# Q, K and V of an attention layer as three products of rounded halves in place of fp32 products

## The chip, the cores and the metric

The kernel is one program on one core of a Trainium2 chip. It is timed in device microseconds (us) of that core; the number that counts is the median of several executions.

## What is computed

Two decoder layers over 256 tokens of width 1024. Layer 0 is a state-space mixer and a dense SwiGLU; layer 1 is a stick-breaking attention (16 heads of 64) and a routed SwiGLU with eight experts, two for each token. Each sub-layer is normalised before and after, and modulated by a vector c. The change touches the projection to Q, K and V:

```python
def stick_breaking_attention(h, w_qkv, w_out):
    qkv = (h @ w_qkv).reshape(bsz, seq, 3, SB_HEADS, SB_HEAD_DIM)
    ...
    z = jnp.einsum("bhqd,bhkd->bhqk", q[:, :, t0:n_keys], k[:, :, :n_keys]) * scale
    ...
    return o @ w_out
```

h is 256 x 1024 and w_qkv is 1024 x 3072, all in fp32.

## The kernel before

All weights come through a ring of seven slots (`ring`, 2 MB each). SyncE issues the loads of the whole kernel in one fixed order (`load`, L485 to L488); a load waits until TensorE has counted `used` for the slot's last content. The granules (one filling of a slot each) that matter here are numbered: 46 to 51 are w_qkv (two for Q, two for K, two for V, 512 columns each), 52 and 53 are the output projection, 54 to 57 the last four of the modulation weights, and from 58 on come the experts' weights. The first five of the experts' granules are loaded without knowing the routing; every later one waits for `route_done` (L550).

The order of each engine's work is written out by hand. Around the change TensorE does this: the last down product of the dense SwiGLU (L2295 to L2308), two modulation products (`ada`, L2336), transposes of the normalised rows (`transpose_x`, L2338), `wait_hT`, then the four granules of Q and K (L2342 to L2354), the two of V (L2355 to L2362), then the heads (L2403 to L2409), the output projection (L2416), modulation, router, gather, and the experts.

- Q and K: for each granule four blocks of 128 output columns, each eight fp32 products over k. The weights are the stationary operand (128 x 128) and `hT`, the transposed activations, is the moving one with 256 columns. That is 128 products, and the profile records each as two loads and two matmuls. The result of a granule stands in banks 0, 1 or 2, 3 of PSUM by turns, and ScalarE copies it to `qT` or `kT` (L890).
- V: for each granule two blocks of 128 tokens, each eight fp32 products with the activations stationary and 512 columns of weights moving: 32 products. VectorE copies them to `v_sb` (L1543).
- Before them ScalarE and VectorE write `hT` (L685 and L1265). ScalarE reads two modulation results (`ada_mod(8)`, `ada_mod(9)`, L712), and loads a table of functions (L886).

The dense SwiGLU before and the experts' main products after are already done the other way. `w_round` (L759 on ScalarE) writes the rounded value of half a granule, as type fp32r, to a buffer; `w_rest` (L1470 on VectorE) writes what the rounding left, over the granule itself (`ring_lo` has the same addresses as `ring`, `x_lo` the same as `hT`); the activations are split the same way (L858, L1514). `split_product` (L2266) then makes one product of three fp32r matmuls: high x high, high x low, low x high.

Of the kernel before, what the change touches and what calls it, by code (L numbers as in the profile page):

```python
# [26 lines left out]
F32 = mybir.dt.float32  # L27
F32R = mybir.dt.float32r
I32 = mybir.dt.int32
U32 = mybir.dt.uint32  # L30
ALU = mybir.AluOpType
ACT = mybir.ActivationFunctionType
AX = mybir.AxisListType

P = 128
D = 1024
KD = D // P
SEQ = 256
TT = SEQ // P
# [7 lines left out]
DH = 64  # L47
# [7 lines left out]
RING = 7  # L55
GRAN = 4096
# [6 lines left out]
G_BANK, U_BANK, T_BANK, S_BANK, Y_BANK = 0, 1, 2, 3, 4  # L63
# [44 lines left out]
N_QKV = 46  # L108
# [29 lines left out]
def program(nc, x, c, ada_w, ada_b, norm_g, s5_w_in, s5_lambda_re, s5_lambda_im, s5_b_re, s5_b_im,  # L138
# [3 lines left out]
    with ctx:  # L142
        def sb(name, shape, dt=F32):
            return ctx.enter_context(nc.sbuf_tensor(name, shape, dt))

        def sem(name):
            return ctx.enter_context(nc.semaphore(name))

        ps = ctx.enter_context(nc.psum_tensor("ps", [P, 8, 512], F32))
# [10 lines left out]
        half = sb("half", [P, 1])  # L160
# [14 lines left out]
        with ExitStack() as first:  # L175
            ring, hT, gg, junk, tbuf, arena = (first.enter_context(nc.sbuf_tensor(name, shape, F32)) for name, shape in (
                ("ring", [P, RING, GRAN]), ("hT", [P, KD, SEQ]), ("gg", [P, D]), ("junk", [P, D]), ("tbuf", [P, D]),
                ("arena", [P, ARENA])))
        with ExitStack() as second:
            def sb2(name, shape):  # L180
                return second.enter_context(nc.sbuf_tensor(name, shape, F32))

            ring_lo = [sb2(f"ring_lo{i}", [P, GRAN]) for i in range(RING)]
            x_lo = sb2("x_lo", [P, KD, SEQ])
            sb2("rows_between", [P, 3 * D])
            w_hi, x_hi = sb2("w_hi", [P, 2, GRAN]), sb2("x_hi", [P, KD, SEQ])
            aT_hi, aT_lo = sb2("aT_hi", [P, 2, 4, P]), sb2("aT_lo", [P, 2, 4, P])
        sb("ring_kept", [P, RING, GRAN])
        w3 = sb("w3", [P, 3, GRAN // 2])
        x3_hi, x3_lo = sb("x3_hi", [P, KD, P]), sb("x3_lo", [P, KD, P])  # L190
# [12 lines left out]
        class Place:  # L203
# [37 lines left out]
        qT, kT, oT = pl(KD, SEQ), pl(KD, SEQ), pl(KD, SEQ)  # L241
# [62 lines left out]
        whi_done, wlo_done, xhi_done, xlo_done, ahi_done = (  # L304
            sem("whi_done"), sem("wlo_done"), sem("xhi_done"), sem("xlo_done"), sem("ahi_done"))
        qk_done, v_out = sem("qk_done"), sem("v_out")
        z_ps, zabs_done, zcopy_done, exp_done, ln_done, sp_done, spm_done = (
            sem("z_ps"), sem("zabs_done"), sem("zcopy_done"), sem("exp_done"), sem("ln_done"), sem("sp_done"),
            sem("spm_done"))
# [57 lines left out]
        def gran(n):  # L367
            return ring[:, n % RING, :]

        def gran8(n):  # L370
            return gran(n).rearrange("p (k n) -> p k n", k=KD)
# [4 lines left out]
        def wait_landed(eng, n, turn=None):  # L376

            eng.wait_ge(landed[n % RING], 16 * (n // RING if turn is None else turn) + 16)

        def wait_used(eng, n, turn=None):  # L380

            eng.wait_ge(used[n % RING], (n // RING if turn is None else turn) + 1)

        def ff_half(buffer, half):
            return buffer[:, 2048 * half:2048 * half + 2048]
# [40 lines left out]

        def half3(h):
            return w3[:, h % 3, :]

        def pair_kinds(eng):  # L430

# [219 lines left out]
        def _(act):  # L651
# [27 lines left out]
            def hT_evict(s, parts=(0, 1, 4, 5)):  # L679

                act.wait_ge(mod_done, s + 1)
                for k in parts:
                    act.wait_ge(hT_ps, 4 * s + k // 2 + 1)
                    dst, src = turned(s, k)
                    act.activation(dst, src, ACT.Identity, bias=shift_col(s, k), scale=scale_c[:, s, k:k + 1]  # L685
                                   ).then_inc(hT_act, 1)
# [22 lines left out]
            def ada_mod(i):  # L709

                act.wait_ge(mod_ps, i + 1)
                act.activation(modc[:, i // 6, 2 * (i % 6):2 * (i % 6) + 2, :],  # L712
                               ps[:, ada_bank(i), 0:8].rearrange("p (q r) -> p r q", r=2), ACT.Copy
                               ).then_inc(mod_out, 1)
# [166 lines left out]
            pre_stats(2)  # L881
            ada_part(9)
            hT_evict(2)
            ada_mod(8)
            ada_mod(9)
            act.preload_act_table_set("natural_log_exp_and_others")  # L886
            for r in range(4):
                wait_used(act, N_QKV + r)
                src = ps[:, 2 * (r % 2):2 * (r % 2) + 2, :].rearrange("p a (b n) -> p (a b) n", b=2)
                act.activation((qT if r < 2 else kT)[:, 4 * (r % 2):4 * (r % 2) + 4, :], src, ACT.Copy,  # L890
                               scale=DH ** -0.5 if r < 2 else 1.0).then_inc(qk_done, 1)
            def o_out(h):
                act.wait_ge(o_ps, h + 1)
                act.activation(oT[:, h, :], ps[:, 6 + h % 2, 0:256], ACT.Copy).then_inc(o_done, 1)
# [325 lines left out]
        def _(dve):  # L1220
# [316 lines left out]
            to_hT(2)  # L1537
            hT_evict(2)

            for n in range(2):  # L1540
                wait_used(dve, N_QKV + 4 + n)
                for tt in range(TT):
                    dve.tensor_copy(v_sb[:, tt, 512 * n:512 * n + 512], ps[:, Y_BANK + 2 * tt + n, :]  # L1543
                                    ).then_inc(v_out, 1)
# [507 lines left out]
        def _(pe):  # L2052
# [51 lines left out]
            def wait_hT(s):  # L2104
                pe.wait_ge(hT_act, 4 * s + 4)
                pe.wait_ge(hT_dve, 4 * s + 4)
# [159 lines left out]
            def split_product(dst, stationary, moving, start, stop):  # L2266

                for i, (a, b) in enumerate(((0, 0), (0, 1), (1, 0))):
                    ins = pe.matmul(dst, stationary[a].bitcast(F32R), moving[b].bitcast(F32R),  # L2269
                                    start=start and i == 0, stop=stop and i == 2)  # L2270
                return ins
# [67 lines left out]
            ada_fold(8)  # L2339
            ada_fold(9)  # L2340
            wait_hT(2)
            for r in range(4):  # L2342
                n = N_QKV + r
                wait_landed(pe, n)
                above(pe, qk_done, r - 1)
                if r == 0:
                    pe.wait_ge(gg_done, 2)
                for j in range(4):
                    if r == 0 and j == 2:
                        pe.wait_ge(mod_out, 10)  # L2350
                    for k in range(KD):
                        ins = pe.matmul(ps[:, 2 * (r % 2) + j // 2, 256 * (j % 2):256 * (j % 2) + 256],  # L2352
                                        gran8(n)[:, k, P * j:P * j + P], hT[:, k, :], start=k == 0, stop=k == KD - 1)
                ins.then_inc(used[n % RING], 1)  # L2354
            for r in range(2):  # L2355
                n = N_QKV + 4 + r
                wait_landed(pe, n)
                for tt in range(TT):
                    for k in range(KD):
                        ins = pe.matmul(ps[:, Y_BANK + 2 * tt + r, :], tokens(k, tt), gran8(n)[:, k, :],  # L2360
                                        start=k == 0, stop=k == KD - 1)
                ins.then_inc(used[n % RING], 1)  # L2362

            def scores(h):

# [680 lines left out]
```

## Time and profile before

| | |
|---|---|
| median of 3 executions | 1531.9 us (1530.35 to 1533.28) |
| the profiled execution | 1534.63 us, its span 1532.9 us |
| TensorE matmuls busy | 1383.5 us (90%) |
| TensorE weight loads busy | 976.7 us (64%) |
| VectorE busy | 661.3 us (43%) |
| ScalarE busy | 498.7 us (33%) |
| moved by DMA | 474.28 MB, mean 309 GB/s |
| mean granted clock of TensorE | 0.949 of 2.4 GHz |

The span runs from the first to the last instruction; the execution's own time is 1.7 us longer. A matmul's recorded duration includes its passage through the array, so its real cost in a row of many is the distance between two starts. "busy" is the union of the recorded spans. A granted clock of 1.00 means 2.4 GHz, 0.50 means 1.2 GHz.

### The profile page before, as it was taken

The numbers are of one execution on the slowest core, as the hardware profiler recorded it, in microseconds if no ns is written. First come the engines' busy times: TensorE is split into PE (matmuls) and PEld (weight loads), VectorE is DVE, ScalarE is ACT, GpSimd is POOL, SyncE is SP. The second block draws the span as 40 slices with busy tenths as digits, with TensorE's granted clock in tenths as the row PEclk, the third lists the DMA queues.
The fourth block names the chain that finished last, engine by engine and source line by source line (L and its number), as shares of the span: only waits on it lengthen the run. The fifth ranks groups of instructions, "written<-read, shape, count | busy, mean of one in ns | idle before, by whom it ended". The sixth has DMA issues, their size and how long they took to land.

```text
span 1532.9 us, 25160 instructions
## 1 busy us (share of the span) xinstructions
PE 1383.5 (90%) x11083; PEld 976.7 (64%) x11084; DVE 661.3 (43%) x755; ACT 498.7 (33%) x557; POOL 34.8 (2%) x66
## 2 busy tenths in 40 slices
PE   3999999999999789899999899999797888988687
PEld 2763788888686545677777577767575565544343
DVE  5943444454400634765544555544665353200003
ACT  2323433434300512444443354433454352000001
POOL 2001000000100002000000000000000000000000
PEclk8989999999999998999999999999998899999889
DMA  8784884554664114559999969999989999999994
GB/s 296 298 316 176 314 346 165 196 188 169 244 246 165 55 51 170 204 216 410 411 411 413 406 234 410 412 410 414 410 340 412 411 412 413 410 411 413 412 413 171
DMA packets 206792, 474.28 MB, mean 309 GB/s; under 512 B 9986, under 2 KB 10030, under 8 KB 206670
## 3 DMA queue, kind: packets, MB, share of 16 engines
q1 hardware_dynamic: 199968, 470.83, 79.0%
q10 hardware_dynamic: 6702, 1.71, 0.5%
q8 instruction: 91, 1.49, 0.4%
q14 instruction: 31, 0.25, 0.0%
HBM read 471.47 MB, written 1.05 MB: 308 GB/s over the span
## 4 chain that ended last, share of the span: by engine, by line
PE 66%; DMA 14%; SPq 11%; DVE 4%; ACT 2%; issue 1%; ACTq 1%; POOL 0%; DVEq 0%
PE ps L2269 34%; SPq L488 11%; DMA ring<-in_moe_w_down_dram 10%; PE ps L2550 7%; PE ps L2562 5%; PE ps L2352 4%; DMA ring<-in_moe_w_gate_up_dram 2%; DMA ring<-in_ada_w_dram 2%; PE ps L2416 2%; PE ps L2245 2%; PE ps L2360 2%; PE ps L2080 2%; DVE ring_lo L1836 1%; DVE arena L1235 1%; PE ps L2144 1%
## 5 line engine op out<-in xcount | busy, mean ns | idle before, releaser
L1836 DVE TENSOR_TENSOR ring_lo<-ring,w 128x2048 fp32r<-128x2048 f32 x126 | 288.4, 2289 | 196.1 <-ACT w L1005 154.1
L1005 ACT ACTIVATE w<-ring 128x2048 fp32r<-128x2048 f32 x126 | 240.6, 1913 | 233.4 <-PE ps L2269 209.3
L2550 PE MATMUL ps<-ring,arena 128*32 128x128 f32 (+1 forms) x5376 | 253.2, 299 | 40.6 <-DMA ring<-in_moe_w_gate_up_dram 32.8
L2550 PEld LDWEIGHTS ps<-ring,arena 128*32 128x32 f32 (+1 forms) x5376 | 189.8, 117 | 104.7 <-issue 45.0
L2269 PE MATMUL ps<-ring_lo,x_hi 128*128 128x512 f32 x560 | 219.4, 392 | 0.0
L2269 PE MATMUL ps<-w,x_hi 128*128 128x512 f32 x336 | 136.4, 406 | 7.1 <-DVE arena L1783 5.5
L1475 DVE TENSOR_TENSOR ring_lo<-ring,w_hi 128x2048 fp32r<-128x2048 f32 x42 | 95.6, 2290 | 85.9 <-ACT w_hi L765 85.9
L2269 PE MATMUL ps<-w,x_lo 128*128 128x512 f32 x336 | 132.1, 393 | 0.0
L2269 PEld LDWEIGHTS ps<-ring_lo,x_hi 128*128 128x128 f32 x560 | 105.9, 189 | 20.3
L2562 PE MATMUL ps<-ring,tri 128*32 128x512 f32 (+1 forms) x448 | 75.7, 693 | 28.0 <-DMA ring<-in_moe_w_down_dram 26.5
L765 ACT ACTIVATE w_hi<-ring 128x2048 fp32r<-128x2048 f32 x42 | 78.8, 1909 | 50.3 <-PE ps L2269 42.1
L2269 PE MATMUL ps<-w_hi,x_hi 128*128 128x512 f32 x224 | 89.4, 399 | 0.0
L2269 PEld LDWEIGHTS ps<-w,x_hi 128*128 128x128 f32 x336 | 63.8, 190 | 37.4 <-issue 18.2
L2269 PE MATMUL ps<-w_hi,x_lo 128*128 128x512 f32 x224 | 87.3, 390 | 0.0
L2269 PE MATMUL ps<-w,a_hi 128*128 128x512 f32 x168 | 69.9, 416 | 2.8 <-DVE a_lo L1871 2.8
L2269 PEld LDWEIGHTS ps<-w,x_lo 128*128 128x128 f32 x336 | 63.6, 189 | 13.7
L2269 PE MATMUL ps<-ring_lo,a_hi 128*128 128x512 f32 x168 | 67.0, 399 | 0.0
L2269 PE MATMUL ps<-w,a_lo 128*128 128x512 f32 x168 | 66.7, 397 | 0.0
L2562 PE MATMUL ps<-ring,arena 128*32 128x512 f32 (+1 forms) x336 | 53.6, 615 | 9.9 <-DMA ring<-in_moe_w_down_dram 7.7
L2080 PE MATMUL ps<-ring,c 128*32 128x512 f32 x384 | 50.4, 678 | 13.1 <-DMA ring<-in_ada_w_dram 12.8
L2562 PEld LDWEIGHTS ps<-ring,tri 128*32 128x32 f32 (+1 forms) x448 | 18.8, 125 | 60.5 <-DMA ring<-in_moe_w_down_dram 30.1
L2352 PE MATMUL ps<-hT,ring 128*128 128x256 f32 x256 | 57.2, 387 | 0.0
(391 smaller groups left out, 1560.6 us busy)
## 6 DMA issues: line engine op xcount, KB each, us to landing
ring<-in_moe_w_gate_up_dram SPq DMA_DIRECT2D x112, 2048.0 KB, 17.2
ring<-in_moe_w_down_dram SPq DMA_DIRECT2D x56, 2048.0 KB, 18.2
ring<-in_ada_w_dram SPq DMA_DIRECT2D x24, 2048.0 KB, 10.8
ring<-in_ffn_w_gate_up_dram SPq DMA_DIRECT2D x14, 2048.0 KB, 12.2
ring<-in_ffn_w_down_dram SPq DMA_DIRECT2D x7, 2048.0 KB, 7.9
ring<-in_sb_w_qkv_dram SPq DMA_DIRECT2D x6, 2048.0 KB, 8.6
ring<-in_s_w_out_dram SPq DMA_DIRECT2D x2, 2048.0 KB, 7.7
ring<-in_sb_w_out_dram SPq DMA_DIRECT2D x2, 2048.0 KB, 13.7
```

Source lines behind the costliest of these rows:

```text
L488: sp.dma_start(dst, src).then_inc(landed[n % RING], 16)
L765: act.activation(ff_half(w_hi[:, g % 2, :], half).bitcast(F32R), ff_half(gran(ff_place(g)), half), ACT.Copy).then_inc(whi_done, 1)
L1005: act.activation(half3(h).bitcast(F32R), ff_half(gran(pair_place(*main_granule(n))), half), ACT.Copy).then_inc(whi_done, 1)
L1475: dve.tensor_tensor(ff_half(ring_lo[(ff_place(g)) % RING][:, :], half).bitcast(F32R), w, ff_half(w_hi[:, g % 2, :], half), ALU.subtract).t ...
L1836: dve.tensor_tensor(ff_half(ring_lo[place % RING][:, :], half).bitcast(F32R), ff_half(gran(place), half), half3(h), ALU.subtract).then_inc ...
L2080: ins = pe.matmul(ps[32 * j:32 * j + 32, ada_bank(i), :], c32[:, 4 * part_k + k, :], gran8(places[r])[:, 4 * part_k + k, :], start=k == 0, ...
L2245: ins = pe.matmul(ps[:, 2 * i + half, :], yT[:, k, P * tt:P * tt + P], gran4(WOUT_PLACES[half])[:, k, 512 * n:512 * n + 512], start=k == 0 ...
L2269: ins = pe.matmul(dst, stationary[a].bitcast(F32R), moving[b].bitcast(F32R), start=start and i == 0, stop=stop and i == 2)
L2352: ins = pe.matmul(ps[:, 2 * (r % 2) + j // 2, 256 * (j % 2):256 * (j % 2) + 256], gran8(n)[:, k, P * j:P * j + P], hT[:, k, :], start=k == ...
L2360: ins = pe.matmul(ps[:, Y_BANK + 2 * tt + r, :], tokens(k, tt), gran8(n)[:, k, :], start=k == 0, stop=k == KD - 1)
L2550: ins = pe.matmul(dst[width * r:width * r + width, 0:cols], x[:, k, 0:width], weights[:, k, cols * r:cols * r + cols], start=k == 0, stop= ...
L2562: ins = pe.matmul(ps[width * r:width * r + width, bank, :], a[:, j, 0:width], weights[:, j, 512 * h:512 * h + 512], start=first and i == 0 ...
```

## The change

Each granule of w_qkv is split in halves of four k each (twelve halves, numbered 0 to 11), and eleven of them are done with three fp32r matmuls in place of an fp32 product. Half 0 (k 0 to 3 of Q's first granule) stays plain fp32. Half 1 is the first split one. Rounded halves go by turns to `wq0` and `wq1`, two new buffers of 2048 columns in space that is free before the heads; what the rounding left is written over the granule. ScalarE writes `x_hi` and the rounded weights, VectorE `x_lo` and the rests. `x_lo` for k 0 to 3 lies over `hT`, so it waits until the plain half has been read (`plain_done`). The two `ada_mod` and the load of the table come later in ScalarE's order. The results of Q and K now stand in four banks each, 4 to 7 and 0 to 3 by turns, so V (in banks 4 to 7) waits for the third copy to `kT`.

```diff
@@ scalar
             hT_evict(2)
+            act.wait_ge(hT_act, 12)
+            act.wait_ge(hT_dve, 12)
+            def q_x(half):
+                k = slice(4 * half, 4 * half + 4)
+                act.activation(x_hi[:, k, :].bitcast(F32R), hT[:, k, :], ACT.Copy).then_inc(q_xhi, 1)
+            def q_round(h):
+                n, half = divmod(h, 2)
+                wait_landed(act, N_QKV + n)
+                if h >= 3:
+                    if half:
+                        wait_used(act, N_QKV + n - 1)
+                    else:
+                        act.wait_ge(q_half, n - 1)
+                act.activation(half_q(h).bitcast(F32R), ff_half(gran(N_QKV + n), half), ACT.Copy).then_inc(q_whi, 1)
+            q_x(1)
+            q_round(1)
+            q_x(0)
             ada_mod(8)
             ada_mod(9)
-            act.preload_act_table_set("natural_log_exp_and_others")
-            for r in range(4):
+            def qk_out(r):
                 wait_used(act, N_QKV + r)
...
+            for h in range(2, 12):
+                q_round(h)
+                if h % 2 and h < 10:
+                    qk_out((h - 3) // 2)
+                if h == 2:
+                    act.preload_act_table_set("natural_log_exp_and_others")
@@ vector
             hT_evict(2)
+            def q_x_rest(half):
+                k = slice(4 * half, 4 * half + 4)
+                dve.wait_ge(q_xhi, 2 - half)
+                if not half:
+                    dve.wait_ge(plain_done, 1)
+                dve.tensor_tensor(x_lo[:, k, :].bitcast(F32R), hT[:, k, :], x_hi[:, k, :], ALU.subtract).then_inc(q_xlo, 1)
+            def q_rest(h):
+                dve.wait_ge(q_whi, h)
+                dve.tensor_tensor(low_q(h).bitcast(F32R), ff_half(gran(N_QKV + h // 2), h % 2), half_q(h), ALU.subtract
+                                  ).then_inc(q_wlo, 1)
+            q_x_rest(1)
+            q_rest(1)
+            q_x_rest(0)
+            for h in range(2, 12):
+                q_rest(h)
@@ tensor
             for r in range(4):
-                n = N_QKV + r
-                wait_landed(pe, n)
+                wait_landed(pe, N_QKV + r)
                 above(pe, qk_done, r - 1)
...
-                    for k in range(KD):
-                        ins = pe.matmul(ps[:, 2 * (r % 2) + j // 2, 256 * (j % 2):256 * (j % 2) + 256],
-                                        gran8(n)[:, k, P * j:P * j + P], hT[:, k, :], start=k == 0, stop=k == KD - 1)
-                ins.then_inc(used[n % RING], 1)
+                base = 0 if r % 2 else Y_BANK
+                for half in range(2):
+                    if r + half:
+                        hi, low = q_weights(2 * r + half)
+                        pe.wait_ge(q_xlo, 1 if r == 0 else 2)
+                    for j in range(4):
+                        for i in range(KD // 2):
+                            k = KD // 2 * half + i
+                            dst, cols_j = ps[:, base + j, 0:256], slice(P * j, P * j + P)
+                            if r + half:
+                                ins = split_product(dst, (hi[:, i, cols_j], low[:, i, cols_j]),
+                                                    (x_hi[:, k, :], x_lo[:, k, :]), k == 0, k == KD - 1)
+                            else:
+                                ins = pe.matmul(dst, gran8(N_QKV)[:, k, cols_j], hT[:, k, :], start=k == 0, stop=False)
...
             for r in range(2):
-                n = N_QKV + 4 + r
...
+                pe.wait_ge(qk_done, 3)
+                for half in range(2):
+                    hi, low = q_weights(8 + 2 * r + half)
+                    for tt in range(TT):
+                        for i in range(KD // 2):
+                            k = KD // 2 * half + i
+                            t = slice(P * tt, P * tt + P)
+                            ins = split_product(ps[:, Y_BANK + 2 * tt + r, :], (x_hi[:, k, t], x_lo[:, k, t]),
+                                                (hi[:, i, :], low[:, i, :]), k == 0, k == KD - 1)
+                    q_read(ins, 4 + r, half)
```

## Rows read from the trace of the kernel before

**Rows 1.** The page, 40 slices of the span: busy share of DMA, and its GB/s.

```profile
DMA  8784884554664114559999969999989999999994
GB/s 296 298 316 176 314 346 165 196 188 169 244 246 165 55 51 170 204 216 410 411 411 413 406 234 410 412 410 414 410 340 412 411 412 413 410 411 413 412 413 171
```

**Rows 2.** Busy time of each engine by stretch (us from the start: length, engines).

```profile
core 0: us, PE busy (x) PEld busy (x) DVE busy (x) ACT busy (x) POOL busy (x), PEclk, DMA share, GB/s
418.50:475.70 57.20, 57.20 (x258) 50.09 (x258) 0.00 (x0) 4.53 (x5) 0.23 (x1) 0.97 0.61 224
475.70:503.00 27.30, 27.30 (x65) 11.81 (x63) 1.29 (x2) 1.02 (x1) 0.00 (x0) 1.00 0.43 154
503.00:551.00 48.00, 33.49 (x225) 26.35 (x224) 36.01 (x52) 28.21 (x40) 0.00 (x0) 0.89 0.12 45
```

**Rows 3.** The chain that ended last, longest pieces, from QKV on: start, us, what.

```profile
418.54 57.17 PE ps L2352 x256
475.71 27.47 PE ps L2360 x64
551.07 8.83 PE ps L2416 x16
561.62 20.61 PE ps L2416 x48
```

**Rows 4.** Issues of the DMA queue by time: start, us, queue.

```profile
380.94 35.54 SPq L488 DMA_DIRECT2D ring<-in_sb_w_qkv_dram  x6
416.52 18.15 SPq L488 DMA_DIRECT2D ring<-in_sb_w_out_dram  x2
503.20 82.98 SPq L488 DMA_DIRECT2D ring<-in_moe_w_gate_up_dram  x4
```

**Rows 5.** What the DMA queue waited for, whole span: us, times, longest.

```profile
SPq L457 <- DVE cnt_i L1710: 31.3, 1, 31.3
```

**Rows 6.** TensorE in order of time, last 32 matmuls of Q and K.

```profile
468.64 7.07 PE L2352 MATMUL ps<-hT,ring 128*128 128x256 f32 x32
```

**Rows 7.** The chain in the dense SwiGLU: runs of fp32r matmuls, 512 columns each.

```profile
262.55 27.53 PE ps L2269 x120
290.52 5.50 PE ps L2269 x24
```

**Rows 8.** TensorE matmuls and weight loads (PEld) in order of time, same stage.

```profile
386.18 0.39 PE L2269 MATMUL ps<-w_hi,aT_hi 128*128 128x512 f32 x1
386.19 0.19 PEld L2269 LDWEIGHTS ps<-ring_lo,aT_hi 128*128 128x128 f32 x1
386.41 0.39 PE L2269 MATMUL ps<-ring_lo,aT_hi 128*128 128x512 f32 x1
```

**Rows 9.** The chain, fp32 matmuls narrow enough that the loads set the pace.

```profile
878.12 3.52 PE ps L2505 x32
```

**Rows 10.** The same 128 narrow matmuls' weight loads: ns min, median, max; times; form.

```profile
L2505 PEld LDWEIGHTS ps<-arena,hn x128: 186/192/192, 645.6 to 1319.1; 128*128 128x128 f32 x128
```

**Rows 11.** The chain, a run of fp32r matmuls in the experts' stage.

```profile
786.68 5.67 PE ps L2269 x24
```

**Rows 12.** Rounding and rest instructions of the dense SwiGLU: ns min, median, max; times; form.

```profile
L858 ACT ACTIVATE x_hi<-hT x2: 1058/1059/1060, 161.3 to 163.3; 128x1024 fp32r<-128x1024 f32 x2
L1514 DVE TENSOR_TENSOR x_lo<-hT,x_hi x2: 1225/1226/1226, 162.4 to 164.4; 128x1024 fp32r<-128x1024 f32 x2
L765 ACT ACTIVATE w_hi<-ring x42: 1895/1909/1919, 118.0 to 382.8; 128x2048 fp32r<-128x2048 f32 x42
L1475 DVE TENSOR_TENSOR ring_lo<-ring,w_hi x42: 2284/2292/2295, 120.0 to 385.2; 128x2048 fp32r<-128x2048 f32 x42
```

**Rows 13.** Copies of Q and K, and of V: ns min, median, max; times; form.

```profile
L890 ACT ACTIVATE arena<-ps x4: 1023/1023/1023, 434.3 to 475.7; 128x1024 f32<-128x1024 f32 x4
L1543 DVE COPY arena<-ps x4: 681/686/692, 489.5 to 503.8; 128x512 f32<-128x512 f32 x4
```

**Rows 14.** The chain, a rounding followed by its rest in the experts' stage.

```profile
1080.46 1.92 ACT w L1005
1082.40 4.50 DVE ring_lo L1836 x2
```

**Rows 15.** ScalarE in order of time where Q's first product starts.

```profile
418.57 0.18 ACT L712 ACTIVATE modc<-ps 128x8 f32<-128x8 f32 x1 [0.28 <-PE ps L2090]
418.77 1.28 ACT L886 ACT_TABLE_LOAD   x1
```

More of the change, by code:

```diff
@@ L187, in program, with sb3 @@
             aT_hi, aT_lo = sb2("aT_hi", [P, 2, 4, P]), sb2("aT_lo", [P, 2, 4, P])
+        with ExitStack() as third:
+            def sb3(name, shape):
+                return third.enter_context(nc.sbuf_tensor(name, shape, F32))
+            sb3("before_o", [P, RING * GRAN + KD * SEQ + 3 * D + 2 * KD * SEQ])
+            wq0 = sb3("wq0", [P, GRAN // 2])
+            sb3("values_third", [P, 2 * KD * SEQ])
+            wq1 = sb3("wq1", [P, GRAN // 2])
         sb("ring_kept", [P, RING, GRAN])
@@ L306, in program @@
         qk_done, v_out = sem("qk_done"), sem("v_out")
+        q_xhi, q_xlo, q_whi, q_wlo, q_half, plain_done = (
+            sem("q_xhi"), sem("q_xlo"), sem("q_whi"), sem("q_wlo"), sem("q_half"), sem("plain_done"))
         z_ps, zabs_done, zcopy_done, exp_done, ln_done, sp_done, spm_done = (
@@ L428, in half3, with half_q, low_q @@
             return w3[:, h % 3, :]
+        def half_q(h):
+            return (wq0, wq1)[h % 2][:, :]
+        def low_q(h):
+            return ff_half(ring_lo[(N_QKV + h // 2) % RING][:, :], h % 2)
         def pair_kinds(eng):
@@ L883, in _ @@
             hT_evict(2)
+            act.wait_ge(hT_act, 12)
[15 more added lines that the diff above has]
+            q_x(0)
             ada_mod(8)
             ada_mod(9)
-            act.preload_act_table_set("natural_log_exp_and_others")
-            for r in range(4):
+            def qk_out(r):
                 wait_used(act, N_QKV + r)
-                src = ps[:, 2 * (r % 2):2 * (r % 2) + 2, :].rearrange("p a (b n) -> p (a b) n", b=2)
-                act.activation((qT if r < 2 else kT)[:, 4 * (r % 2):4 * (r % 2) + 4, :], src, ACT.Copy,
-                               scale=DH ** -0.5 if r < 2 else 1.0).then_inc(qk_done, 1)
+                base = 0 if r % 2 else Y_BANK
+                act.activation((qT if r < 2 else kT)[:, 4 * (r % 2):4 * (r % 2) + 4, :], ps[:, base:base + 4, 0:256],
+                               ACT.Copy, scale=DH ** -0.5 if r < 2 else 1.0).then_inc(qk_done, 1)
+            for h in range(2, 12):
[4 more added lines that the diff above has]
+                    act.preload_act_table_set("natural_log_exp_and_others")
             def o_out(h):
@@ L2341, in _, with q_weights, q_read @@
             wait_hT(2)
+            def q_weights(h):
+                pe.wait_ge(q_wlo, h)
+                return [w.rearrange("p (k n) -> p k n", n=512) for w in (half_q(h), low_q(h))]
+            def q_read(ins, n, half):
+                ins.then_inc(used[(N_QKV + n) % RING] if half else q_half, 1)
             for r in range(4):
-                n = N_QKV + r
-                wait_landed(pe, n)
+                wait_landed(pe, N_QKV + r)
                 above(pe, qk_done, r - 1)
-                if r == 0:
+                if r == 1:
@@ L2347, in _ @@
                     pe.wait_ge(gg_done, 2)
-                for j in range(4):
-                    if r == 0 and j == 2:
-                        pe.wait_ge(mod_out, 10)
-                    for k in range(KD):
-                        ins = pe.matmul(ps[:, 2 * (r % 2) + j // 2, 256 * (j % 2):256 * (j % 2) + 256],
-                                        gran8(n)[:, k, P * j:P * j + P], hT[:, k, :], start=k == 0, stop=k == KD - 1)
-                ins.then_inc(used[n % RING], 1)
-            for r in range(2):
-                n = N_QKV + 4 + r
[L2357 to L2362, printed above, removed]
+                    pe.wait_ge(mod_out, 10)
@@ new lines, in _ @@
+                base = 0 if r % 2 else Y_BANK
+                for half in range(2):
[11 more added lines that the diff above has]
+                                ins = pe.matmul(dst, gran8(N_QKV)[:, k, cols_j], hT[:, k, :], start=k == 0, stop=False)
+                    if r + half:
+                        q_read(ins, r, half)
+                    else:
+                        ins.then_inc(plain_done, 1)
```

## The prediction

> **What bounds the kernel now.** I read the slices of the page first. From the nineteenth slice on the DMA engines move some 410 GB/s almost without a pause: the experts' stage is tied to the stream of weights. In slices 14 and 15, the heads, they move 55 and 51 GB/s [rows 1]: there the stream waits for TensorE. So the question is whether time saved at Q, K and V moves the start of the late stream, or is swallowed by it. The busy times by stretch answer the first half: from 418.5 to 503.0 us TensorE is busy all the time, VectorE nearly idle (0.00 and 1.29 us), ScalarE 4.53 and 1.02 us, and DMA at 0.61 and 0.43 [rows 2]. The chain of waits says the same: it runs through all 57.17 us of Q and K and all 27.47 us of V, then through the heads and the output projection [rows 3]. The DMA queue answers the second half: the six granules of w_qkv are issued by 416.5 us, and the first of the experts' loads goes out at 503.20 us, when V's last product is done; the fourth and later ones follow the output projection [rows 4]. The loads after the fifth wait 31.3 us for the routing, which VectorE computes at the end of the chain [rows 5]. Nothing after V is tied to an absolute time. A microsecond taken from Q, K and V is a microsecond off the end, the heads and everything behind them simply start earlier.
>
> **Q and K, matmuls.** Before: 128 products, 256 recorded matmuls, 57.17 us [rows 3]. The last 32 records take 7.07 us from the first start to the last end; less 0.38 us for the last one's passage, 31 distances of 0.216 us [rows 6]. 256 of these are 55.3 us; the other 1.9 us are the start of the stage, at a granted clock of 0.97 on average [rows 2], and stay, since the first products are the same. After: the 16 plain products of half 0 are 32 records, 6.9 us, with the start 8.8 us. The other 112 products are 336 fp32r matmuls of 256 columns. No row shows an fp32r matmul as narrow as that, so this price is bounded from both sides. In the dense SwiGLU 120 fp32r matmuls of 512 columns take 27.53 us, 24 take 5.50 us: 0.229 us each [rows 7]; two successive starts lie 0.23 us apart [rows 8]. 512 columns at 2.4 GHz would be 0.213, so 0.016 us come on top, whether per matmul or per column is open. With 256 columns the stream is 0.107 us, and with all of the 0.016 on top 0.123. From below, the pace of the loads is a floor: 32 fp32 matmuls of 64 columns, each with a load of 128 x 128, take 3.52 us, 0.110 us each, though their own two passes need only 0.053 [rows 9]. I take 0.121, near the upper end, as part of the 0.016 (the seams between groups) should not repeat with each matmul: 336 x 0.121 = 40.7 us. The floor of 0.110 gives 37.0. Under the traffic of the experts' stage the wide ones take 5.67 / 24 = 0.236 us [rows 11], 0.007 more; 0.130 for the narrow ones is the upper bound, 43.7 us.
>
> **V, matmuls.** Before: 32 products, 27.47 us [rows 3]. After: 96 fp32r matmuls of 512 columns, the form that rows show: 96 x 0.229 = 22.0 us [rows 7], at most 96 x 0.236 = 22.7 [rows 11].
>
> **Sum.** Before 57.17 + 27.47 = 84.6 us; after 8.8 + 40.7 + 22.0 = 71.5. That is 13.1 us less: 7.7 from Q and K, 5.4 from V. By the bounds the gain is 16.8 (floor of the loads) to 9.4 us (both upper prices).
>
> The page "TensorE: Matmul & The Clock Gate" of the Trainium skill gives, under "Back-to-back issue gap", N / 2.4 + 2.5 ns for N columns. That would be 0.216 us at 512 columns, and the fp32r rows are 0.013 over it [rows 7], so the trace doesn't agree for this type; by the page the two stages would save 18.4 us, an estimate from its formula.
>
> **The split operands, what hides them.** None of ScalarE's and VectorE's new work is on the path as long as it is done before TensorE asks. I count from TensorE's first product. The durations are those of the same instructions in the dense SwiGLU: `x_hi` 1.06 us, `x_lo` 1.23, rounding of half a granule 1.91, its rest 2.29 [rows 12].
> - ScalarE: `x_hi` for k 4 to 7 until 1.1, rounding of half 1 until 3.0, `x_hi` for k 0 to 3 until 4.1, then the two `ada_mod` at 0.18 each, rounding of half 2 until 6.4, then the table, 1.28 [rows 12, 15].
> - VectorE: `x_lo` until 2.4, rest of half 1 until 5.4. TensorE wants it at 8.8: 3.4 us of cover. Then `x_lo` for k 0 to 3 waits for the plain half; VectorE stands in that wait with the rest of half 2 queued behind it: 8.8 + 1.2 + 2.3 = 12.4. TensorE wants it when half 1 is done, at 8.8 + 48 x 0.121 = 14.6: 2.2 us of cover.
> - From half 3 on a buffer is free when TensorE has done the half two before, and rounding and rest must be done within the half between: 1.91 + 2.29 = 4.2 us and the handovers, against 5.8 us for Q and K (48 matmuls) and 24 x 0.229 = 5.5 for V. A rest follows its rounding by 0.02 us [rows 14]; with some 0.1 to 0.3 us for each signal to and from TensorE the margin is about 1 us.
> - The copies of Q and K (1.02 us [rows 13]) stand behind a rounding in ScalarE's order, so they come 1.9 us later than they could. The copy of a granule is asked for one granule later (11.6 us), V needs the third one while the fourth granule is being worked on: covered. If the cover were gone, each would cost about 1.0 us. V's copies stand behind the last rest, which is done some 4.5 us into V's second granule, so they too are ready; the last pair is at the very end, as before.
> - `ada_mod(8)` and `ada_mod(9)` come 4.1 us later. Behind them wait the GpSimd's sum, not wanted for long, and TensorE before Q's second granule, at 14.6 us. Zero. The extra waits of ScalarE for `hT` are those that TensorE ends anyway. No DMA is moved in SyncE's order, and the slots come free once per granule as before, only sooner; w_qkv is issued by 416.5 us, so the third granule has landed long before about 445 us, when it is wanted.
>
> **Rivals.**
> 1. *The weight loads come out from under the short matmuls* (slower). An fp32r product needs three loads for 256 columns each; before, two for the same number of columns twice. If a load kept TensorE for its recorded 0.188 to 0.192 us [rows 10], 336 matmuls would take 0.19 us: 23.2 us more than in my sum, 10 us slower than before, about 1542. If loads and streams simply followed one another, 0.110 + 0.107 = 0.217 each, it would be 32 us over my sum, 1551. It decides for slower from 0.160 us per matmul on (13.1 / 336 = 0.039 over 0.121). Against it: the loads with 192 ns on record follow at 0.110 us [rows 9, 10], and a load starts 0.01 us after the matmul before it starts, long before that one ends [rows 8]. For it: no row has an fp32r load under a stream as short as the load itself. The Trainium skill, "TensorE: Matmul & The Clock Gate", section "Part 3: Packing small matmuls", says that a load overlaps a running matmul only if it aims at other rows of the array; by that rule this rival would be the outcome, and [rows 8] speak against the rule.
> 2. *The narrow fp32r matmul takes as long as the wide one.* Then 336 x 0.229 = 76.9, 36 us over my sum: 1555. The fp32 rows scale with the columns: 0.216 us for 256, 27.47 / 64 = 0.429 for 512 [rows 3, 6]. For fp32r nothing in the trace shows the scaling.
> 3. *The rounding is the bound.* If signals, or ScalarE and VectorE being slower beside TensorE's reading, stretch the 4.2 us to 6.6 per half of Q and K, each of eight halves or so costs 0.8 and V's four 1.1: 11 less 0.1, about 1529. A stretch to 6.0 costs 4 us. Against: the same instructions took at most 1.92 and 2.30 us beside the same matmuls [rows 12].
> 4. *The gain is taken back later*, if the late stream starts by something else than TensorE: 1530 to 1533. [rows 4, 5] speak against.
>
> **How the numbers follow.** Profiled execution: span 1532.9 - 13.1 = 1519.8, time 1534.63 - 13.1 = 1521.5. The median stood 2.7 us under the profiled one, so 1531.9 - 13.1 = 1518.8. Chances: forecast 0.68 (1515 to 1522.5 by its bounds), rival 1 0.09 (0.06 at 1542, 0.03 at 1551), rival 2 0.06, rival 3 0.10, rival 4 0.07. The forecast with its spread and that of the executions reaches from 1514 to 1524; rival 3 and a part of rival 4 are taken in up to 1530, which leaves rivals 1 and 2 out and holds about 0.8. A measurement can tell 0.2%, 3 us, from no change. Faster by more than that: forecast and most of rival 3, 0.77. Within: rival 4 and the rest, 0.08. Slower: rivals 1 and 2, 0.15.
>
> **What would show it.** In the profile after: 336 matmuls of 256 columns on `split_product`'s line, about 0.12 us apart; rest of half 2 ended before half 1; no idle time of TensorE put down to the new rests between 418 and 490 us; V's 96 at 0.229; the first of the experts' loads at about 490 us in place of 503.20, and the end as much earlier. What would make it wrong is the narrow fp32r matmul above all: each 0.01 us is 3.4 us of the end. Next is a margin at the buffers smaller than 1 us, seen as idle time every half.

## The result

The changed kernel takes 1520.32 us (median of 5, 1517.84 to 1523.64) against 1533.28 us before (median of 5, 1530.35 to 1536.14). The ratio is 0.9907, 95% interval 0.9892 to 0.9922: a gain of under 1%, but clear of the scatter. The profiled execution has a span of 1518.6 us, 14.3 us less than before. In a second set beside other kernels the ratio was 0.9908 (0.9892 to 0.9925), and the span of the profile 1520.8 us.

The chain of waits of the changed kernel, its long pieces from the stage on (start, us, what), to be read beside [rows 3]:

```profile
421.27 8.82 PE ps L2433 x32
430.09 62.09 PE ps L2332 x432
539.97 7.13 PE ps L2502 x16
548.82 20.61 PE ps L2502 x48
```

L2433 is the plain half, L2332 `split_product`: Q, K and V are 8.82 + 62.09 = 70.9 us in place of 57.17 + 27.47 = 84.6. That is 13.7 us. The stretches of the changed kernel are the plain half, the split part of Q and K, and V (columns as in [rows 2]):

```profile
421.20:430.10 8.90, 8.90 (x35) 7.53 (x35) 3.52 (x2) 7.01 (x7) 1.26 (x1) 0.81 1.05 407
430.10:470.50 40.40, 40.40 (x338) 40.36 (x338) 17.18 (x8) 14.23 (x10) 0.00 (x0) 1.00 0.61 227
470.50:492.30 21.80, 21.80 (x98) 17.80 (x98) 8.15 (x6) 6.66 (x4) 0.00 (x0) 1.00 0.54 193
```

TensorE has no pause in any of the three. In the middle one the weight loads count as busy for 40.36 of 40.40 us too. That alone doesn't make them the limit: each is recorded with 0.19 us, and where one starts every 0.120 us the records overlap and fill the whole stretch. VectorE and ScalarE, nearly idle there before, now work 28.8 and 27.9 us under TensorE. The matmuls and loads of `split_product` between 430 and 492 us (times in ns, min, median, max), and what TensorE waited for at them:

```profile
L2332 PE MATMUL ps<-x_hi,wq x112: 280/283/472, 429.7 to 469.9; 128*128 128x256 f32 x112
L2332 PEld LDWEIGHTS ps<-x_lo,wq x112: 187/192/192, 429.9 to 469.9; 128*128 128x128 f32 x112
L2332 PE MATMUL ps<-wq,x_hi x32: 389/389/396, 470.2 to 491.3; 128*128 128x512 f32 x32
its engine sat idle before it (us, times) until:
who waited for it (us, times):
  ACT wq L916: 34.1, 9
```

Under "sat idle" stands nothing. The loads are recorded with 192 ns, like those of [rows 10], but the 336 matmuls came 40.4 / 336 = 0.120 us apart. The DMA queue shows that what follows moved along. The first of the experts' loads goes out at 492.22 us, against 503.20 us in [rows 4]:

```profile
383.66 35.60 SPq L504 DMA_DIRECT2D ring<-in_sb_w_qkv_dram  x6
492.22 81.17 SPq L504 DMA_DIRECT2D ring<-in_moe_w_gate_up_dram  x4
```

One profile alone can mislead by 1 to 3 us. Here the stage began 2.7 us later than before, in code that the change doesn't touch; the stage gave 13.7; what follows it was 3.3 us shorter (1026.4 against 1029.7 us). In the second profile the same three are 1.5, 13.7 and -0.2. The stage is the same to 0.1 us, the rest scatters. Only one part of the rest was the same in both: the output projection ran at a granted clock of 1.00 in place of 0.95 and took 29.5 in place of 31.2 us. These are its stretches, before and changed:

```profile
551.07:582.20 31.13, 31.13 (x72) 13.46 (x76) 1.22 (x1) 0.00 (x0) 0.00 (x0) 0.95 0.19 68
```

```profile
539.97:569.40 29.43, 29.43 (x72) 12.89 (x76) 1.23 (x1) 0.00 (x0) 0.00 (x0) 1.00 0.20 72
```

In the kernel before, the granted clock was 1.00 in the last 2 us of the heads, and 0.65 and then 0.50 in the first two stretches of 2 us of the projection; in the changed kernel it stayed at 1.00. The first 16 matmuls of the projection took 7.13 us in all three profiles that have the changed kernel's Q, K and V unaltered ahead of them (the third is that of the last experiment), and 8.2 to 9.3 us in the nine others, one of which is the changed kernel with 20 us of other work put before Q. So the 1.7 us repeat, but whether the change brings them, by the moment at which it lets the projection start, no run says. They can't be told in the time either: behind the projection the two profiles of the changed kernel have 949.2 and 952.8 us against 950.7 before, and the medians gained 13.0 and 13.4 us, while the interval of the first ratio (12.0 to 16.5 us) holds 13.7 + 1.7 too.

### The profile page after: what moved, and what is told of

Its sections match the earlier page's. It is cut to its first block, busy times and chain, and to the rows that moved or that the text cites. A ratio compares the mean times of both kernels' runs of the same rounds, so it can differ in the third digit from the quotient of the medians.

```text
span 1518.6 us, 25494 instructions
## 1 busy us (share of the span) xinstructions
PE 1370.0 (90%) x11227; PEld 981.0 (65%) x11228; DVE 688.5 (45%) x768; ACT 521.2 (34%) x570; POOL 35.8 (2%) x66
## 3 DMA queue, kind: packets, MB, share of 16 engines
q8 instruction: 92, 1.51, 0.4%
## 4 chain that ended last, share of the span: by engine, by line
PE 65%; DMA 15%; SPq 11%; DVE 4%; ACT 2%; issue 2%; ACTq 1%; POOL 0%; DVEq 0%
PE ps L2332 38%; SPq L504 11%; DMA ring<-in_moe_w_down_dram 11%; PE ps L2636 7%; PE ps L2648 5%; DMA ring<-in_ada_w_dram 2%; DMA ring<-in_moe_w_gate_up_dram 2%; PE ps L2308 2%; PE ps L2502 2%; PE ps L2143 2%; DVE arena L1281 1%; PE ps L2207 1%; DVE ring_lo L1899 1%; PE ps L2591 1%; PE ps L2268 1%
## 5 line engine op out<-in xcount | busy, mean ns | idle before, releaser
L2332 PE MATMUL ps<-ring_lo,x_hi 128*128 128x512 f32 x592 | 231.8, 392 | 0.0
L2332 PE MATMUL ps<-w,x_hi 128*128 128x512 f32 x336 | 136.7, 407 | 4.8 <-DVE arena L1846 4.6
L2332 PE MATMUL ps<-w,x_lo 128*128 128x512 f32 x336 | 132.1, 393 | 0.0
L2332 PEld LDWEIGHTS ps<-ring_lo,x_hi 128*128 128x128 f32 x592 | 111.9, 189 | 21.7 <-issue 0.2
L2332 PE MATMUL ps<-w_hi,x_hi 128*128 128x512 f32 x224 | 89.4, 399 | 0.0
L2332 PE MATMUL ps<-w_hi,x_lo 128*128 128x512 f32 x224 | 87.3, 390 | 0.0
L2332 PEld LDWEIGHTS ps<-w,x_hi 128*128 128x128 f32 x336 | 63.7, 190 | 34.3 <-issue 16.0
L2332 PEld LDWEIGHTS ps<-w,x_lo 128*128 128x128 f32 x336 | 63.7, 189 | 13.8
L2332 PE MATMUL ps<-w,a_hi 128*128 128x512 f32 x168 | 69.5, 413 | 2.8 <-DVE a_lo L1934 2.8
L2332 PE MATMUL ps<-w,a_lo 128*128 128x512 f32 x168 | 66.5, 396 | 0.0
L2332 PE MATMUL ps<-ring_lo,a_hi 128*128 128x512 f32 x168 | 66.5, 396 | 0.0
L2143 PE MATMUL ps<-ring,c 128*32 128x512 f32 x384 | 49.9, 673 | 13.7 <-DMA ring<-in_ada_w_dram 13.5
L2648 PEld LDWEIGHTS ps<-ring,tri 128*32 128x32 f32 (+1 forms) x448 | 19.1, 128 | 61.9 <-issue 31.2
L1854 DVE TENSOR_TENSOR c<-c,ps 128x128 f32<-128x128 f32 (+1 forms) x28 | 8.8, 314 | 96.6 <-PE ps L2636 96.6
```

Source lines behind the costliest of these rows:

```text
L2143: ins = pe.matmul(ps[32 * j:32 * j + 32, ada_bank(i), :], c32[:, 4 * part_k + k, :], gran8(places[r])[:, 4 * part_k + k, :], start=k == 0, ...
L2648: ins = pe.matmul(ps[width * r:width * r + width, bank, :], a[:, j, 0:width], weights[:, j, 512 * h:512 * h + 512], start=first and i == 0 ...
```

## The experiments

The theory: each of the two terms (narrow fp32r matmuls in Q and K, wide ones in V) has its price, the rounding is covered, and the whole passes 1:1 to the end. The main rivals: the narrow form or its loads are dear; the plain half isn't needed; the rounding has no margin; later stages take part of the gain back. Where a gain is given beside a ratio, with an interval, it is 1 less the ratio, times the some 1535 us of the kernel before.

**Q and K alone.** V goes back to fp32 products (from the rounded activations, the low part left out).

```diff
-            for h in range(2, 12):
+            for h in range(2, 8):
                 q_rest(h)
...
+                        ins = pe.matmul(ps[:, Y_BANK + 2 * tt + r, :], x_hi[:, k, P * tt:P * tt + P], gran8(n)[:, k, :],
+                                        start=k == 0, stop=k == KD - 1)
```

> Only Q and K are split; V is computed as fp32 products again, from the rounded activations alone (its low part is left out, so V's numbers are coarser). Theory (the two terms of the sum stand alone and pass 1:1 to the end): V's stage takes 27.5 us as before the change, Q and K 49.1 us as in the changed kernel; the time is 5.7 us above the changed kernel's and 7.3 to 8 us under the kernel before. Rival (the gain comes from elsewhere, the later stages in a luckier phase of the clock): the time doesn't follow the stage, the difference to the kernel before is not 7 to 9 us but near 0 or near 13.

```profile
419.31 8.82 PE ps L2434 x32
428.13 40.31 PE ps L2333 x336
468.44 27.47 PE ps L2445 x64
```

The chain has the three parts as expected, 76.6 us, 8.0 less than before. The time: 1528.07 us against 1534.83, ratio 0.9949 (0.9931 to 0.9967), which is 7.8 us (5.1 to 10.6).

**V alone.** Q and K stay fp32; the low part of the activations goes to other space, so nothing is overwritten that Q and K read.

```diff
-                if not half:
-                    dve.wait_ge(plain_done, 1)
-                dve.tensor_tensor(x_lo[:, k, :].bitcast(F32R), hT[:, k, :], x_hi[:, k, :], ALU.subtract).then_inc(q_xlo, 1)
+                dve.tensor_tensor(x_lov[:, k, :].bitcast(F32R), hT[:, k, :], x_hi[:, k, :], ALU.subtract).then_inc(q_xlo, 1)
...
+                            ins = pe.matmul(dst, gran8(N_QKV + r)[:, k, cols_j], hT[:, k, :], start=k == 0, stop=k == KD - 1)
```

> Only V is split; Q and K are fp32 products as before the change (in the four banks each of the changed kernel), and the low part of the activations lies in other space. Theory: Q and K take 57.2 us, V 21.8 us, and the time is 5.4 to 5.7 us under the kernel before. Together with the run that splits Q and K alone the two gains add up to the whole, 13 to 14 us. Rival: they don't add up, since one of them hides the other's rounding: then V alone would stall for its weights and gain under 4 us.

```profile
419.51 57.17 PE ps L2424 x256
476.68 21.78 PE ps L2330 x96
```

57.17 + 21.78 us, no pause before V. Ratio 0.9969 (0.9956 to 0.9983), 4.8 us (2.6 to 6.8) where the stage gives 5.7. In the stage the two gains add up exactly, 8.0 + 5.7 = 13.7; in the times 7.8 + 4.8 = 12.6, within their intervals.

**Half 0 split as well.** No plain half covers the first rounding.

```diff
+            q_x(0)
+            q_round(0)
             q_x(1)
             q_round(1)
-            q_x(0)
```

> Half 0 is split too, so no plain half covers the first rounding. Theory (the plain half is a cover): TensorE stands still for 1.06 + 1.9 + 2.3 = 5.3 us at the start, then works 5.8 us, 11.1 against 8.8 us for the plain half: 2.3 us more than the changed kernel, and up to 1 us more if the clock falls in the pause. Rival (the cover is not needed, other work of ScalarE and VectorE is what TensorE would wait for anyway, and the 32 fp32 records are the dearer way): 8.8 less 5.8, up to 3 us less than the changed kernel.

TensorE's first matmuls after the pause, and the stretch that follows (clock in the column before the last two):

```profile
425.07 0.55 PE L2332 MATMUL ps<-x_hi,wq 128*128 128x256 f32 x1 [5.42 <-DVE ring_lo L1594]
425.42 0.41 PE L2332 MATMUL ps<-x_lo,wq 128*128 128x256 f32 x1
425.63 0.41 PE L2332 MATMUL ps<-x_hi,ring_lo 128*128 128x256 f32 x1
425.84 0.41 PE L2332 MATMUL ps<-x_hi,wq 128*128 128x256 f32 x1
425.00:495.70 70.70, 70.63 (x482) 66.63 (x484) 27.33 (x15) 24.45 (x18) 0.59 (x1) 0.96 0.58 210
```

The pause is 5.4 us, as worked out. But the matmuls after it took 70.56 us, and 62.09 + 5.76 = 67.85 would be their price at full clock; the clock was 0.96. So the stage is 76.0 us, 5.1 over the changed kernel's, not 2.3. The expectation had allowed up to 1 us for the clock; 2.7 us are slow clock. Ratio 0.9963 (0.9952 to 0.9975), 5.7 us under the kernel before.

These 2.7 us are not all the pause's. The stretches of this run (the pause, the slow part) and, in the second fence, of the changed kernel without a pause (just before the stage, its first 3.8 us, the rest of the plain half):

```profile
419.65:425.00 5.35, 0.00 (x0) 0.00 (x0) 3.71 (x3) 5.35 (x4) 0.00 (x0) 0.57 1.05 409
425.00:430.50 5.50, 5.43 (x25) 5.46 (x26) 3.17 (x2) 0.36 (x3) 0.59 (x1) 0.50 1.05 402
```

```profile
419.40:421.20 1.80, 1.80 (x18) 1.78 (x16) 1.76 (x4) 1.56 (x4) 0.00 (x0) 1.00 1.06 413
421.20:425.00 3.80, 3.80 (x11) 3.03 (x11) 2.08 (x2) 3.75 (x4) 0.00 (x0) 0.55 1.06 410
425.00:430.10 5.10, 5.10 (x26) 4.51 (x25) 1.43 (x1) 3.27 (x5) 1.26 (x1) 1.00 1.05 405
```

The clock falls to 1.2 GHz at the start of this stage with and without a pause, in the kernel before too (0.51 from 418.50 to 422.00 us, TensorE busy throughout). The plain half pays 1.9 us for it, 8.82 us where 6.91 are its price at full clock. The pause adds 0.8 us. The 5.1 us are then 5.4 of pause, plus these 0.8, less 1.15, as a split half takes 5.76 us in place of 6.91.

**The pause filled.** To test that the 2.7 us are slow clock and not the operands or the waits, TensorE is kept busy in the pause with products whose result is thrown away.

```diff
             wait_hT(2)
+            for i in range(12):
+                pe.matmul(ps[:, Y_BANK, 0:256], ident[:, :], hn[:, 0, 0:256], start=True, stop=True)
```

> As the run in which all halves are split, but TensorE is kept busy in the pause of 5.4 us by 12 fp32 products of 256 columns whose result is thrown away (24 records, 5.2 us and the cold start). Theory (2.7 us of that run's 76.0 us were a lower clock, which the pause had brought): the 528 matmuls after the pause take 67.9 us in place of 70.6, the stage 73.5 to 75 us. Rival (the 2.7 us come from the operands or from the first half's waits): the stage stays at 76 or gets longer by what the filler runs over.

```profile
418.00 7.01 PE ps L2406 x24
425.01 67.85 PE ps L2332 x480
```

67.85 us, with the clock at 1.00 in that stretch, where 67.9 were expected. So it was the clock. The filler pays for the slow start in its place: 24 records would be 5.2 us at full clock and took 7.0. It runs over the pause by 1.6 us, and still the stage is shorter, 74.9 against 76.0 us. Ratio 0.9942 (0.9925 to 0.9958), 8.9 us (6.5 to 11.5) where the stage gives 9.8. Whatever stands first in this stage pays 1.8 to 1.9 us of slow clock if TensorE works on, and 2.7 us if it pauses first.

**Three roundings in place of one**, from half 3 on.

```diff
+                for i in range(2 if h >= 3 else 0):
+                    act.activation(half_q(h).bitcast(F32R), ff_half(gran(N_QKV + n), half), ACT.Copy).then_inc(again, 1)
+                    act.wait_ge(again, 2 * (h - 3) + i + 1)
                 act.activation(half_q(h).bitcast(F32R), ff_half(gran(N_QKV + n), half), ACT.Copy).then_inc(q_whi, 1)
```

> From half 3 on each rounding is done three times over, 5.8 us in place of 1.9 us, so rounding and rest take 8.2 to 8.5 us of a half that TensorE works on for 5.8 us (5.5 in V). This is the prediction's third rival made real. Theory A, as priced there: every half pays the excess, 9 halves x 2.5 us = 23 us and more over the changed kernel. Theory B: with two buffers the wait goes from one half to the half two before, so a stall at one half gives the next its time, and only every second half pays: 3 x 2.5 + 2 x 2.8 = 13 us, seen as idle times of 2.4 to 3 us at every second half. If the margin were not 1.1 to 1.4 us as the trace has it, both would come out higher or lower by that.

Starts after a pause of TensorE, from its order of time, and its waits from 421 to 510 us in sum:

```profile
444.73 0.39 PE L2336 MATMUL ps<-x_hi,wq 128*128 128x256 f32 x1 [2.53 <-DVE ring_lo L1599]
460.53 0.39 PE L2336 MATMUL ps<-x_hi,wq 128*128 128x256 f32 x1 [2.53 <-DVE ring_lo L1599]
467.33 0.36 PE L2336 MATMUL ps<-x_hi,wq 128*128 128x256 f32 x1 [0.79 <-DVE ring_lo L1599]
```

```profile
PE ps L2336 <- DVE ring_lo L1599: 12.6, 8, 2.5
```

Between the pauses of 2.53 us that end at 444.73 and 460.53 lie two halves of work without one. The sum is theory B's: 12.6 us in all, 13 expected, where theory A asks for 23. Its pattern is not: from 467.33 us on every half pays, in turns less (0.79 to 0.94 us) and more (1.51 to 1.76). What holds is that two halves together pay the excess about once: the matmuls that follow the long pauses start 14.05 to 14.3 us apart from 460.53 us on, and one half of work (5.76) with three roundings and a rest (some 8.2) is 14.0.

The stage is 87.1 us, 16.1 over the changed kernel's. Of the 3.5 us beyond the pauses, 1.8 lie in one place: from 445.90 to 449.20 us the granted clock was 0.50, and the half after the first pause took 7.52 us. After the second pause, just as long, it took 6.03 us at a clock of 1.00. Time 1541.3 us (three executions), ratio 1.0045 (1.0015 to 1.0074): 6.9 us slower (2.3 to 11.4), where the stage says 2.4.

**Narrower still.** Each low product as two matmuls of 128 columns.

```diff
+                                w, xs = (hi[:, i, cols_j], low[:, i, cols_j]), (x_hi[:, k, :], x_lo[:, k, :])
+                                pe.matmul(dst, w[0].bitcast(F32R), xs[0].bitcast(F32R), start=k == 0, stop=False)
+                                for a, b in ((0, 1), (1, 0)):
+                                    for c in range(2):
+                                        t = slice(P * c, P * c + P)
+                                        ins = pe.matmul(dst[:, t], w[a].bitcast(F32R), xs[b][:, t].bitcast(F32R),
+                                                        start=False, stop=k == KD - 1 and a + c == 2)
```

> In Q and K each of the two low products is done as two fp32r matmuls of 128 columns in place of one of 256; the high product stays at 256. 112 wide and 448 narrow ones. Theory (a stream of columns plus a fixed 0.013 us, with the pace of the loads, 0.112 us, as the floor): the narrow ones lie 0.112 us apart, Q and K's split part takes 112 x 0.120 + 448 x 0.112 = 63.6 us in place of 40.3. Rival (an fp32r matmul narrower than 256 columns isn't done in one pass): 128 columns in four passes are 0.213 us, and the part takes 109 us. A third: loads of the same weights in a row are cheaper, then less than 63 us.

```profile
430.60:493.70 63.10, 63.10 (x562) 63.10 (x561) 17.18 (x8) 14.22 (x9) 0.00 (x0) 1.00 0.40 147
```

63.1 us for 560 matmuls, 63.6 expected; 0.113 us each on average. Single starts lie closer (from this run's order of time: starts of matmuls of 128 columns, then of loads):

```profile
440.17 0.23 PE L2435 MATMUL ps<-x_lo,wq 128*128 128x128 f32 x1
440.23 0.27 PE L2435 MATMUL ps<-x_lo,wq 128*128 128x128 f32 x1
440.34 0.39 PE L2435 MATMUL ps<-x_hi,ring_lo 128*128 128x128 f32 x2
```

```profile
439.82 0.19 PEld L2435 LDWEIGHTS ps<-x_hi,ring_lo 128*128 128x128 f32 x1
439.94 0.19 PEld L2431 LDWEIGHTS ps<-x_hi,wq 128*128 128x128 f32 x1
440.05 0.31 PEld L2435 LDWEIGHTS ps<-x_lo,wq 128*128 128x128 f32 x2
```

Two starts are 0.06 us apart, which leaves no room for four passes of 128 columns (0.213), nor for two (0.107). The matmuls come 0.06 to 0.17 us apart, the loads evenly every 0.11 to 0.12, and 0.113 is near the 0.110 of [rows 9], where the loads set the pace too. So it is the pace of the loads that keeps a narrow fp32r matmul from being cheaper, not the number of passes. The stage is 93.7 us, 9.1 over the kernel before; the one execution of this kernel took 1548.35 us, 12.9 over the median beside it.

**20 us of filler** before Q, in the changed kernel (as above, 46 products).

> The changed kernel with 46 fp32 products of 256 columns, whose result is thrown away, before the first product of Q: 92 records x 0.216 us = 19.9 us more on TensorE, all other work as it is. Theory (what the stage gains or loses passes 1:1 to the end): 19.9 us over the changed kernel, so 6 to 7 us over the kernel before. Rival (the stream of weights takes part of it up): under 15 us over the changed kernel, so no slower than the kernel before.

The chain has 21.63 us of filler, then 6.91 us for the plain half, which now starts at full clock, and 62.09 as before. The stage is 90.6 us, 6.0 over the kernel before; the ratio 1.0048 (1.0033 to 1.0063) is 7.4 us (5.1 to 9.7). What the stage loses, the end loses, and the stream of weights takes none of it up that could be told.

**The changed kernel again, and half 0 split again.**

> The changed kernel once more, beside the others of this set. Theory (the stage passes 1:1 to the end): 12 to 14 us under the kernel before. Rival (part of the gain is given back later and the first result was lucky): 9 to 11 us. The runs with only Q and K split, only V split, and all split gave 6.8, 4.7 and 5.3 us where their stages had gained 8.0, 5.7 and 8.6.

Ratio 0.9908 (0.9892 to 0.9925), medians 1521.99 and 1535.42 us, 13.4 us apart: the first result (13.0) is repeated.

> The run with all halves split once more, since its time (5.3 us under the kernel before) was 3.3 us more than its stage (76.0 against 84.6 us) explains. Theory (scatter of the start and of the experts' stages, 2 us each way): 7 to 9.5 us under the kernel before this time. Rival (the pause costs something later as well): 4 to 6 us under it again.

Ratio 0.9958 (0.9945 to 0.9970), 6.5 us (4.6 to 8.5), between the two expectations; the medians are 7.8 us apart. The stage gives 9.0 this time: the same pause of 5.43 us, and 70.17 us of matmuls, so the slow clock costs 2.3 us where it had cost 2.7. In both its runs this kernel is 2 to 3 us slower than its stage says; the two profiles have 1032.2 and 1031.7 us behind the stage against 1029.7 before. No run says what these 2 us are.

**The output projection split too**, with the same plain half as a cover.

```diff
+            for tt in range(TT):
+                for k in range(KD // 2):
+                    ins = pe.matmul(ps[:, Y_BANK + 2 * tt, :], oT[:, k, P * tt:P * tt + P], gran8(N_SBOUT)[:, k, :],
+                                    start=k == 0, stop=False)
+            ins.then_inc(plain_done, 1)
+            gate_row(2)
+            for h in range(1, 4):
+                pe.wait_ge(q_wlo, 11 + h)
+                pe.wait_ge(q_xlo, 3 if h == 1 else 4)
+                for tt in range(TT):
+                    for i in range(KD // 2):
+                        ins = s_product(h // 2, h % 2, tt, i)
```

> The changed kernel, and the output projection of the attention is done the same way: its first half granule (k 0 to 3) plain as a cover, three halves as three fp32r matmuls of 512 columns. By the terms that held at V, 24 products at 0.858 us become 72 matmuls at 0.227: 20.6 to 16.4 us, 4.2 us less than the changed kernel. The rounding of the activations and of half 1 takes some 5.4 us from the last head on and is covered by the plain half (6.9 us) and the row of gates (1.7 us). Rival: the last head's rest comes late and TensorE waits; then the gain is 1 to 2 us less, and an idle time shows before the first split half.

```profile
537.90 7.13 PE ps L2554 x16
545.03 1.72 PE ps L2222 x4
546.75 16.38 PE ps L2379 x72
```

25.2 us in place of the changed kernel's 29.5, and 16.38 where 16.4 was worked out; no idle time before the split halves. 1518.12 us (1516.74 to 1518.66) beside 1521.99 us for the changed kernel in the same set (1521.31 to 1522.67); ratio to the kernel before 0.9882 (0.9865 to 0.9898). This version is the fastest of the three. It is 3.9 us under the changed kernel by the medians, and the projection had gained 4.2.

## Why the prediction was right, point by point

- *The sum.* Forecast 1518.8 us and 13.1 us less; measured 1520.32 and 13.0 less (the kernel before was 1.4 us slower in this set than the median forecast from). The terms: plain half with its start 8.8, measured 8.82; the narrow matmuls 40.7, measured 40.3; V 22.0, measured 21.8. The price that no row showed, 0.121 us between bounds of 0.110 and 0.130, is 0.120. That is 0.107 for the columns and 0.013 on top, and at 512 columns in V (21.78 / 96 = 0.227) it is 0.013 again: the surplus goes by the matmul, and the rest of the 0.229 of [rows 7] doesn't repeat with each, as the prediction had argued. It shows at 2.4 GHz only: in the run with all halves split the matmuls from 425.42 to 430.32 us, at a clock of 0.50, start 0.213 us apart, which is 256 columns at 1.2 GHz and nothing on top.
- *The cover.* The rest of half 1 was ready 3.7 us before TensorE wanted it (3.4 foretold), that of half 2 2.2 us (2.2), later ones 1.4 us in Q and K and 1.1 in V (about 1). The copies and the later `ada_mod` cost nothing: no wait on TensorE names them. The 1.9 us of slow start, which the prediction kept in its 8.8, are the clock, and they were there as said; a pause in place of the plain half would have made them 2.7.
- *The passage to the end.* Right in size. Stages that gained 13.7, 8.0, 5.7 and 9.8 us and one that lost 6.0 gave gains of 14, 7.8, 4.8 and 8.9 and a loss of 7.4 in the times, all within their intervals. But each of the three runs in which TensorE stands still in the stage comes out short by 2.5 to 4.5 us (both with all halves split, and the one with three roundings). With the pause filled the shortfall is 0.9. That a pause costs something behind the stage as well isn't shown by this: the one execution with narrower matmuls, which had no pause, is 3.8 us short too. What these few us are stays open.
- *Rival 1 (loads come out).* Fallen: no idle time, loads under every matmul, and 560 narrow matmuls at the loads' own pace. The Trainium skill's rule ("TensorE: Matmul & The Clock Gate", "Part 3: Packing small matmuls") that a load overlaps only matmuls on other rows of the array is contradicted by these runs, in which both are 128 x 128 and a matmul starts every 0.120 us; the same section also lets a load go ahead if it aims at a background weight buffer, and that would fit them, though no run shows that it is this. By the same page of the Trainium skill ("LDWEIGHTS"), 128 / 1.2 = 107 ns for a load of 128 columns is an estimate near the 0.113 us measured.
- *Rival 2 (a narrow fp32r matmul costs as much as a wide one).* Fallen: 0.120 against 0.227 to 0.229.
- *Rival 3 (rounding as the bound).* It didn't occur, and its price was wrong in two ways. It charged the excess to eight halves of Q and K, though by the prediction's own list only those from half 3 on wait for a buffer, which are five. And it charged it to each half, where the run with three roundings shows that two halves together pay it once. With its 0.8 and 1.1 us of excess that makes 4 to 5 us in place of 11, an estimate. The step that failed is to take the time of a turn as the time between two stalls.
- *Rival 4.* Nothing was taken back that could be told: the filler run and the two sets say so, within some 2 us. Single profiles scatter by up to 3 us before and behind the stage, so that spans alone would have given 14.3 us once and 12.1 us the other time.

## What to carry to other kernels

Before an fp32 product is replaced by three rounded ones, compare three prices per product: the streams, the pace of the loads (0.112 us each) and the surplus of 0.013 us per matmul. With 512 columns that gives 0.68 against 0.86 us, with 256 columns 0.36 against 0.43, and at 128 the three loads (0.34) would cost more than the fp32 product, which by the loads' pace is 2 x 0.112 = 0.22, an estimate. Cover the first rounding with work on TensorE that is needed anyway and doesn't wait for it. A pause there costs its length, and here up to 0.8 us of slow clock on top. With two buffers, an excess of rounding over a half's work is paid about once for every two halves. Take the gain of a stage from the stage's own time, in several profiles.

## What the runs showed of the hardware

- An fp32r matmul of 128 columns is done in one pass: starts down to 0.06 us apart. The loads of 128 x 128 that go with them start every 0.112 to 0.113 us, though each is recorded with 0.19. A busy share of loads near 1 is therefore no sign that they are the limit: it was 40.36 of 40.40 us at 0.120 us per matmul too.
- The surplus of 0.013 us per fp32r matmul, the same at 256 and 512 columns, shows at 2.4 GHz and is gone at 1.2 GHz (0.213 us for 256 columns).
- The granted clock fell to its lower level at the start of this stage with TensorE busy in the 1.8 and 2.5 us before it (0.51 and 0.55 in the stretches that follow), as well as in a pause of 5.4 us (0.57). Work that came at once lost 1.8 to 1.9 us by it, work after the pause 2.7 and 2.3 us. Of two pauses of 2.53 us in one run, one was followed by 3.3 us at 0.50 and the other by none.
- The clock at the start of the output projection stayed high in three profiles and fell in nine: 7.13 us, or 8.2 to 9.3, for the same 16 matmuls.
